# Hybrid attention block: earlier first products, head mix two tiles ahead, reordered GpSimd and load work around the switch of token halves

## The chip, the cores and the metric

The kernel runs on one core of a Trainium2 chip. The metric is device time in microseconds (us), the median of several executions. A core has a matrix engine (TensorE, PE in the rows; its weight loads are PEld), three engines for elementwise work (VectorE or DVE, ScalarE or ACT, GpSimd or POOL), and SyncE (SP, its queue is SPq), which here issues nearly all transfers between HBM and the on-chip memory. Each engine works through its own instructions in order. They meet only at semaphores: `wait_ge` holds an engine, and with it everything behind in its order, until a count is reached.

## The reference, cut to what matters

One layer on x, 2048 tokens of width 1024, all in float32:

- h = rmsnorm(x) times a gain; a projection with 2304 + 8 columns;
- eight heads of sliding window attention with sinks, and eight heads of causal attention with a cumulative forget gate, from these columns;
- x = x + mixed heads times w_out;
- h = rmsnorm(x) times a gain; u = relu(h w_up), 4096 wide; x = x + (u*u) w_down;
- a last rmsnorm.

Float32 accuracy is kept by splitting each operand of a product into a high part (rounded to the fast format) and the rest, and by three fast products: hi*hi, hi*lo, lo*hi. ScalarE makes each high part by a copy, VectorE makes the rest by a subtraction. The MLP uses a scheme of seven products of half blocks in place of eight, whose operands are sums and differences of blocks, made on GpSimd.

## The kernel before, in words

**Front (`project`, lines 182 to 653).** The 16 tiles of 128 tokens run through: load into a ring of four slots (line 318; slot reuse waits for the turn of the tile four before), square with sum on ScalarE (`square`, L399), two tiny operations on GpSimd for 1/rms (L384, L389), scaling on VectorE (`norm`, L477), eight transposes on TensorE (`turn`, L587), high copy on ScalarE in two halves (`split_ht_hi`, L405), rest on VectorE in two halves (`split_ht_lo`, L484). Four tiles make a token block b. The first two weight chunks of 128 columns give 8 products ("first products", `product_first`, L599), number n being chunk n % 2 on block n // 2, each 24 matmuls of 512 columns. They are put between the turns by `product_after_turn`: before the change numbers 0 to 5 stand after the turns of tiles 5, 7, 9, 11, 13, 15, and 6 and 7 at the end. Each result is read out by `split_first` on ScalarE (L425) and VectorE (L502), put one tile later. Product n waits for the rests of its four tiles; the turn of tile t waits for its scaling and for the rests of tile t-2. The gate weights (8 columns) are turned once (L615) at GATE_TILE. `square` runs one tile ahead, and its unused output goes to a scratch tile, `squares`.

**Head mix (`mix_out`, L1445 on).** Again 16 tiles: SyncE loads the two parts of the heads' output and the factors 1/sum (`load_mix`), GpSimd adds the parts (`join`, L1548), VectorE multiplies (`divide`, L1622), ScalarE and VectorE split (`split_mix`, L1585, L1627), TensorE does 48 matmuls (L1685), VectorE adds x (L1646), then square (L1608), 1/rms (L1570, L1573), scaling (L1653), turn (L1673), and ScalarE copies the turned tile out (`copy_ht`, L1596). From tile 8 on this copy goes to a staging tile that SyncE stores (`store_ht`, L1517), and GpSimd also forms token differences (L1560) in tiles 8 to 13. Two slots hold each of these tiles. SyncE's order in step t is: load_mix(t+2), wait for the add of t, store x_mid, load x(t+2), and from t = 9 store_ht(t-1).

**MLP (`feed`, L1725 on).** The up products go through 32 groups of 256 columns, 16 for each half of the tokens, with seven products (0 to 6) of 12 matmuls each (L2533). The operands of the seven products from the tokens are the "hops". Those of the first half are made at the start. Of the second half, numbers 4, 5 and 6 are made early, stored in HBM (`store_parts`) and loaded back in group 15 (`load_parts`, L1944), numbers 0 to 3 are split in group 15 (L2408). Weight operands are split three products ahead (LEAD = 3): ScalarE L2223, VectorE L2389. GpSimd makes four weight combinations per group (`mix_w` 1 to 4, L2085, L2090, L2092, L2096) and four result sums (`mix_u`, L2114 to L2124). VectorE's `add_up` (L2443) of product 5 stands behind the split of the next group's operand 0; product 6 waits for it: `pe.wait_ge(summed, 3 * g + 2)`. SyncE loads the weights of group g+2 (`load_w`, L1928) and stores seven results per group (L1948). LAST_TILE is the product ahead of which the turn of tile 15 stands.

Of the kernel before, what the change touches and what calls it, by code (L numbers as in the profile page):

```python
# [168 lines left out]
def project(nc, x, norm_mix, w_in, b_forget, sinks, ident_dram, causal_dram, alibi_dram, proj_hi, proj_lo, decay,  # L169
# [12 lines left out]
    with ExitStack() as ctx:  # L182
# [50 lines left out]

        squares = whole.raw["p_o_hi0"][:, S - D:S]
        gate_first = whole.raw["p_o_lo1"][0:G, S - D:S]
# [7 lines left out]
        assert NCH == 2 * PAIRS  # L243
        GATE_TILE = 7
        COPIED = 2 * ST + 1
# [3 lines left out]

        product_after_turn = {t: 2 * (t // TPB - 1) + t % TPB // 2 for t in range(TPB, ST) if t % 2}  # L250
        product_before_turn = {t + 1: n for t, n in product_after_turn.items() if t + 1 < ST}
# [142 lines left out]
        def _(act):  # L394
            def square(t):
                act.wait_ge(x_loaded[t % X_RING], 16 * (t // X_RING + 1))
                if t:
                    act.wait_ge(squared, t)
                nc.scalar.activation(squares, x_in[:, t % X_RING], ACT.Square,  # L399
                                     accum_out=ssum[:, t:t + 1]).then_inc(squared, 1)  # L400

            def split_ht_hi(t):
                for half in range(2):
                    act.wait_ge(turned, 2 * t + half + 1)
                    nc.scalar.activation(  # L405
                        ht_hi[half][:, :, t * P:(t + 1) * P],
                        ps_t[2 * (t % 2) + half].rearrange("p (k s) -> p k s", s=P),
                        ACT.Copy).then_inc(ht_hi_done, 1)
# [9 lines left out]
            def split_first(n):  # L418
                if n == 4:
                    act.wait_ge(squared, ST)  # L420
                split_o_hi(n % 2, n // 2, n % 4, n)
# [16 lines left out]

            square(0)
            for t in range(ST):  # L440
                if t + 1 < ST:
                    square(t + 1)
                if t in product_before_turn:
                    split_first(product_before_turn[t])
                split_ht_hi(t)
                if t == 2:
                    split_w_hi(0)
                    split_w_hi(1)
            for n in range(2 * SB - 3, 2 * SB - 1):
                split_first(n)  # L450
# [20 lines left out]
        def _(dve):  # L471
# [73 lines left out]
            for t in range(ST):  # L545
                if t + 1 < ST:
                    norm(t + 1)
                if t in product_before_turn:
                    split_first(product_before_turn[t])
                split_ht_lo(t)  # L550
                if t == GATE_TILE:
                    scale_gate_weights()
                if t == 2:
                    split_w_lo(0)
                    split_w_lo(1)
            for n in range(2 * SB - 3, 2 * SB - 1):
                split_first(n)
# [20 lines left out]
        def _(pe):  # L578
# [24 lines left out]
            def product_first(n):  # L603
                slot, b = n % 2, n // 2
                pe.wait_ge(ht_lo_done, 2 * TPB * (b + 1))
                pe.wait_ge(w_lo_done, 2)
                if n >= 4:
                    pe.wait_ge(o_lo_done, n - 3)
                product(slot, b, n % 4)
# [835 lines left out]
def mix_out(nc, o_main, o_rest, rsum_inv, x, norm_mlp, w_up, whole, joint, raw, w_raw, hop_hi, hop_lo, x_mid, h_rest,  # L1445
# [6 lines left out]
    with ExitStack() as ctx:  # L1452
# [91 lines left out]
        def _(pool):  # L1544
# [17 lines left out]
            pool.sem_inc(joined, 1)  # L1562
            pool.wait_ge(mhalf_set, 1)
            for t in range(ST):
                if t + 1 < ST:
                    join(t + 1)
                if t == ST - 1:
                    mlp.gpsimd_first(pool)
                pool.wait_ge(squared, t + 1)
                nc.gpsimd.tensor_scalar(rstd[:, t:t + 1], ssum[:, t:t + 1], 1.0 / D, EPS,  # L1570
                                        ALU.mult, ALU.add).then_inc(meaned, 1)
                pool.wait_ge(meaned, t + 1)
                nc.gpsimd.tensor_tensor(rstd[:, t:t + 1], rstd[:, t:t + 1], mhalf[:], ALU.pow).then_inc(rooted, 1)  # L1573
                if KEPT <= t < KEPT + 6:
                    mix_tokens(t - KEPT)
# [3 lines left out]
        def _(act):  # L1579
# [18 lines left out]

            act.sem_inc(mix_hi_done, 1)
            for t in range(ST):  # L1600
                if t + 1 < ST:
                    split_mix(t + 1)
                else:
                    mlp.scalar_first(act)
                act.wait_ge(added, HALVES * (t + 1))
                if t >= 2:
                    act.wait_ge(turned, 2 * (t - 1))
                nc.scalar.activation(xn[:, t % 2], xm[:, t % 2], ACT.Square,  # L1608
                                     accum_out=ssum[:, t:t + 1]).then_inc(squared, 1)
                if t:  # L1610
                    copy_ht(t - 1)
# [6 lines left out]
        def _(dve):  # L1618
# [12 lines left out]
            dve.sem_inc(divided, 1)  # L1631
            dve.sem_inc(mix_lo_done, 1)
            for t in range(ST):
                slot = t % 2
                if t + 1 < ST:
                    divide(t + 1)
                    split_mix(t + 1)
                else:
                    mlp.vector_first(dve)
# [8 lines left out]
                if t == 0:  # L1648
                    dve.wait_ge(gain_in, 16)
                if t == ST - 1:  # L1650
                    mlp.vector_second(dve)
                dve.wait_ge(rooted, t + 1)
                nc.vector.scalar_tensor_tensor(xn[:, slot], xm[:, slot], rstd[:, t:t + 1], gain[:],  # L1653
                                               ALU.mult, ALU.mult).then_inc(normed, 1)
                if t in SPLIT_AT:
                    n = SPLIT_AT.index(t)
# [68 lines left out]
def feed(nc, ctx, x_mid, h_rest, whole, joint, raw, raw_parts, w_raw, hop0_hi, hop0_lo, u_ops, b_kept, t_rest, t_parts,  # L1725
# [140 lines left out]
    hop_at = {0: (0, 4), 1: (0, 5), 3: (0, 6)}  # L1866
    LAST_TILE = 2
    hop_at |= {SWITCH + 1: (1, 0), SWITCH + 2: (1, 1), SWITCH + 5: (1, 2), SWITCH + 6: (1, 3),
# [51 lines left out]
    def sync(sp, store_last_tile):  # L1920
# [11 lines left out]
        def store_token_mix(n):  # L1932
            sp.wait_ge(t_mixed, 1 + 2 * (n + 1))
            sp.dma_start(t_rest[n], raw[:, 1]).then_inc(t_stored, 16)
# [72 lines left out]
        store_last_tile()  # L2007
        for g in range(GROUPS):
            if g:
                store_rest(g - 1)  # L2010
            if g + 2 < GROUPS:
                load_w(g + 2)
            if g == 1:
# [3 lines left out]
                sp.dma_start(raw[:], h_rest.rearrange("p j b k s -> p (j b) k s")).then_inc(raw_in, 16)  # L2017
            if g in rest_stored_at:
                store_token_mix(rest_stored_at[g])
            if g in pre_stored_at:  # L2020
                store_parts(pre_stored_at[g])
            if g == FG - 3:
                sp.wait_ge(t_stored, PRE_STORED)
                for slot, src in enumerate((h_rest[:, 0, 0], t_rest[T1_REST], t_rest[T2_REST], h_rest[:, 1, 0])):
                    sp.dma_start(raw[:, slot], src).then_inc(t_stored, 16)
            if g == FG - 1:
                for i in sorted(PRE_ORDER):
                    load_parts(i)
            if g == FG + 3:
# [76 lines left out]
    def gpsimd(pool):  # L2106
# [59 lines left out]
        for g in range(GROUPS):  # L2166
# [6 lines left out]
            if g == FG - 1:  # L2173
                pool.wait_ge(hop_lo_done, hop_count[1, 1])
            if g:
                mix_u(g - 1)
            if 2 <= g < 10:
                mix_rest(*divmod(g - 2, 2))
            if g + 1 < GROUPS:
                mix_w(g + 1, 3)  # L2180
        mix_u(GROUPS - 1)
# [498 lines left out]
```

## Time and profile before

| | us |
|---|---|
| median of 3 runs (2395.7 to 2396.91) | 2396.8 |
| profiled execution, its own time | 2394.05 |
| its span | 2392.4 |
| TensorE busy in the span | 2326.6 (97%) |
| VectorE busy | 1520.1 (64%) |
| ScalarE busy | 1154.1 (48%) |
| GpSimd busy | 706.9 (30%) |

The span runs from the first to the last instruction; the run's own time is 1.65 us more. TensorE leaves 65.8 us of the span idle, and the change works on places where it is idle.

### The profile page before, as it was taken

To read this page: it belongs to the slowest core of one execution; us is meant where nothing else is said; L and a number is where in the kernel's file an instruction comes from. 1 tells how busy PE (TensorE), PEld (TensorE's weight loads), DVE (VectorE), ACT (ScalarE), POOL (GpSimd) and SP (SyncE) were. 2 spreads that over 40 slices of the span, in tenths; PEclk is the share of its full clock that TensorE was granted. 3 is DMA by queue.
4 is the path that set the end of the run, shared out by engine and by line. 5 is a ranking of instruction groups with operands and counts; after the bars stand their busy time and mean duration, and the time that the engine had idled before them with its cause. 6 is when DMAs were issued, how large, how long until landed. Compare 5 with 4: busy or idle time off the path is not lost.

```text
span 2392.4 us, 34959 instructions
## 1 busy us (share of the span) xinstructions
PE 2326.6 (97%) x11346; PEld 1934.7 (81%) x11346; DVE 1520.1 (64%) x2623; ACT 1154.1 (48%) x2226; POOL 706.9 (30%) x593
## 2 busy tenths in 40 slices
PE   7999999999999998999899999999999999999998
PEld 5888888788888886887687877888888888888887
DVE  6588873688888886566745655444465555564454
ACT  5211112788888886223545555555553233333243
POOL 2000000111111114235568764666640032120132
PEclk9999999999999999999999999999999999999999
DMA  5567765666666565766455576654457486564464
GB/s 189 215 235 278 268 242 163 180 160 156 160 157 157 152 156 169 248 218 202 170 183 163 189 286 242 202 160 152 154 190 260 165 298 234 193 219 162 138 219 160
DMA packets 253970, 469.09 MB, mean 196 GB/s; under 512 B 59336, under 2 KB 119752, under 8 KB 246032
## 3 DMA queue, kind: packets, MB, share of 16 engines
q1 hardware_dynamic: 247808, 451.11, 58.6%
q0 software_dynamic: 6048, 16.52, 2.6%
q8 instruction: 64, 1.05, 0.2%
q14 instruction: 50, 0.41, 0.1%
HBM read 316.13 MB, written 151.42 MB: 195 GB/s over the span
## 4 chain that ended last, share of the span: by engine, by line
PE 51%; DVE 3%; POOL 2%; issue 2%; DMA 1%; ACT 1%; SPq 0%; POOLq 0%; ACTq 0%; DVEq 0%
PE m_ps L2533 24%; PE m_ps L2556 23%; PE m_ps L1685 4%; DMA b_kept<-f_kept 1%; POOL m_mix L1548 1%; DVE f_up_lo L2389 1%; PE m_ps L2574 0%; DVE m_xn L1653 0%; DVE m_xm L1646 0%; DVE m_mix L1622 0%; ACT m_mix_hi L1585 0%; DVE keep_lo L2408 0%; POOL h_raw L1560 0%; POOL f_kept L2157 0%; DVE hop_lo L1659 0%
## 5 line engine op out<-in xcount | busy, mean ns | idle before, releaser
L2556 PE MATMUL m_ps<-keep_hi,hop_hi 128*128 128x512 f32 x880 | 342.5, 389 | 0.4 <-DVE hop_lo L2392 0.4
L2556 PE MATMUL m_ps<-keep_hi,hop_lo 128*128 128x512 f32 x880 | 342.4, 389 | 0.0
L2556 PE MATMUL m_ps<-keep_lo,hop_hi 128*128 128x512 f32 x880 | 342.3, 389 | 0.0
L2392 DVE TENSOR_TENSOR hop_lo<-h_raw,hop_hi 128x512 fp32r<-128x512 f32 x224 | 176.6, 789 | 236.8 <-ACT hop_hi L2228 236.7
L2389 DVE TENSOR_TENSOR f_up_lo<-wide_raw,f_up_hi 128x512 fp32r<-128x512 f32 x160 | 182.5, 1142 | 223.0 <-ACT f_up_hi L2223 222.9
L2228 ACT ACTIVATE hop_hi<-h_raw 128x512 fp32r<-128x512 f32 x224 | 140.8, 630 | 334.4 <-PE m_ps L2556 330.5
L958 POOL DMA_DIRECT2D o_main<-a_o x63 | 36.5, 580 | 775.2 <-ACT a_o L1326 726.6
L599 PE MATMUL p_ps_o<-p_ht_lo,p_w_hi 128*128 128x512 f32 x576 | 224.5, 390 | 0.0
L2533 PE MATMUL m_ps<-keep_hi,f_up_hi 128*128 128x512 f32 x512 | 202.8, 396 | 6.1 <-DVE f_up_lo L2389 4.7
L2533 PE MATMUL m_ps<-keep_hi,f_up_lo 128*128 128x512 f32 x512 | 201.3, 393 | 0.0
L2533 PE MATMUL m_ps<-keep_lo,f_up_hi 128*128 128x512 f32 x512 | 199.4, 390 | 0.0
L2556 PEld LDWEIGHTS m_ps<-keep_hi,hop_hi 128*128 128x128 f32 x880 | 165.2, 188 | 34.8 <-DVE hop_lo L2392 0.8
L2556 PEld LDWEIGHTS m_ps<-keep_hi,hop_lo 128*128 128x128 f32 x880 | 165.2, 188 | 34.6
L2556 PEld LDWEIGHTS m_ps<-keep_lo,hop_hi 128*128 128x128 f32 x880 | 165.2, 188 | 34.3
L425 ACT ACTIVATE p_o_hi<-p_ps_o 128x512 fp32r<-128x512 f32 x70 | 41.8, 598 | 306.7 <-PE p_ps_o L599 299.4
L1199 DVE TENSOR_TENSOR a_pt_lo<-p_ps_o,a_pt_hi 128x512 fp32r<-128x512 f32 (+3 forms) x234 | 142.3, 614 | 15.3 <-ACT a_pt_hi L1313 14.6
L1313 ACT ACTIVATE a_pt_hi<-p_ps_o 128x512 fp32r<-128x512 f32 (+3 forms) x234 | 125.1, 544 | 41.1 <-PE p_ps_o L1085 36.0
L1022 PE MATMUL p_ps_x<-p_o_hi 128*128 128x512 f32 (+2 forms) x320 | 138.2, 432 | 4.4 <-DMA p_o_lo<-proj_lo 1.8
L1111 PE MATMUL p_ps_o<-a_pt_hi,a_v_fox 128*128 128x512 f32 (+1 forms) x320 | 128.9, 403 | 8.1 <-DVE a_pt_lo L1199 7.8
L599 PEld LDWEIGHTS p_ps_o<-p_ht_lo,p_w_hi 128*128 128x128 f32 x576 | 108.4, 188 | 22.4
L515 DVE CUSTOM_DVE_ANT_0 p_ps_x<-wide_raw,p_bias,p_rstd 128x1024 f32<-128x1024 f32 x86 | 116.1, 1350 | 14.8 <-DMA wide_raw<-gate_w 4.4
L2533 PEld LDWEIGHTS m_ps<-keep_hi,f_up_hi 128*128 128x128 f32 x512 | 96.6, 189 | 26.8 <-DVE f_up_lo L2389 7.3
(246 smaller groups left out, 5779.8 us busy)
## 6 DMA issues: line engine op xcount, KB each, us to landing
h_raw<-u_ops SPq DMA_DIRECT2D x224, 256.0 KB, 4.2
wide_raw<-in_w_up SPq DMA_DIRECT2D x32, 1024.0 KB, 7.2
u_ops<-f_u SPq DMA_DIRECT2D x128, 256.0 KB, 4.3
wide_raw<-in_x SPq DMA_DIRECT2D x59, 512.0 KB, 4.0
u_ops<-f_us SPq DMA_DIRECT2D x96, 256.0 KB, 2.3
proj_hi<-p_o_hi SPq DMA_DIRECT2D x17, 1024.0 KB, 6.2
proj_lo<-p_o_lo SPq DMA_DIRECT2D x17, 1024.0 KB, 8.3
h_raw<-in_w_down SPq DMA_DIRECT2D x58, 256.0 KB, 3.9
```

The source lines that it names most:

```text
L515: nc.vector.tensor_tensor_reduce(out=front.pair[:], in0=job_tile(m), in1=x_in[:, 2 + e], scale=rstd[:, t:t + 1], scalar=bias[:, g:g + 1], ...
L599: last = nc.tensor.matmul(ps_o[bank][:], w[:, slot, k, :], h, start=(k == 0 and n == 0), stop=(k == DK - 1 and n == 2))
L1022: last = nc.tensor.matmul(ps_s[ring][:, 0:w], tiles.q_fox[b // 2][:, q], kk[n // 2][:, k], start=(m == 0), stop=(m == 1 and n < b))
L1111: last = nc.tensor.matmul(bank[:, BANK - w:BANK], v_st[kind][:, step[2]], pt[:, 0:w], start=(first and pt is hi), stop=(last_one and pt is ...
L1199: nc.vector.tensor_tensor(pt_lo[i % PT_RING][:, 0:w], bank[:, 0:w], pt_hi[i % PT_RING][:, 0:w].bitcast(F32), ALU.subtract).then_inc(p_lo_d ...
L1313: nc.scalar.activation(pt_hi[i % PT_RING][:, 0:w], bank[:, 0:w], ACT.Copy).then_inc(p_hi_done, 1)
L1685: done = nc.tensor.matmul(joint.banks[2 * (t % 2) + half][:], m, w, start=(first and n == 0), stop=(last and n == 2))
L2228: nc.scalar.activation(op_tiles(m)[0], a_raw[:, q % A_RING], ACT.Copy).then_inc(op_hi_done, 1)
L2389: nc.vector.tensor_tensor(by_k(lo), w_part(m), by_k(hi).bitcast(F32), ALU.subtract).then_inc(op_lo_done, 1)
L2392: nc.vector.tensor_tensor(lo, a_raw[:, (m - UP) % A_RING], hi.bitcast(F32), ALU.subtract).then_inc(op_lo_done, 1)
L2533: last = nc.tensor.matmul(bank[:], w[:, k], h[i][:, k], start=(UP_OPENS[i] and k == 0 and m == 0), stop=(k == 3 and m == 2), skip_group_ch ...
L2556: last = nc.tensor.matmul(down_banks[b % 2][t][:], a[:, cols], w[j], start=(j == 0 and m == 0), stop=(j == FG - 1 and m == 2))
```

## The change

It has four parts. (1) Front: the first products 0 to 5 stand after the turns of tiles 3, 5, 8, 10, 12, 14; the squares of tiles 1 to 3 stand one place earlier in ScalarE's order; the split of the second weight chunk moves from tile 2 to tile 3; the scratch of the squares moves to another tile; the gate tile is 5. (2) Head mix: `join`, `divide` and `split_mix` work on tile t+2 in step t instead of t+1, and on VectorE and ScalarE they stand after the add and the square. (3) LAST_TILE is 3. (4) MLP: token mixes are stored ahead of the weight load; `load_parts(4)` stands at the head of group 15, parts 5 and 6 behind the result stores of group 14, and `load_w(17)` behind them; GpSimd's `mix_w` 3 stands ahead of the token differences, in group 15 also ahead of `mix_u`, which there waits for one hop more.

```diff
-        squares = whole.raw["p_o_hi0"][:, S - D:S]
+        squares = whole.raw["keep_hi"][:].rearrange("p (k b) s -> p k (b s)", k=DK // 2)[:, :, S - 2 * P:S]
-        GATE_TILE = 7
+        GATE_TILE = 5
-        product_after_turn = {t: 2 * (t // TPB - 1) + t % TPB // 2 for t in range(TPB, ST) if t % 2}
+        product_after_turn = {t: n for n, t in enumerate((3, 5, 8, 10, 12, 14))}
...
@@ scalar, front
+                if t == ST - 2:
+                    act.wait_ge(squared, ST)
...
             square(0)
+            square(1)
             for t in range(ST):
-                if t + 1 < ST:
-                    square(t + 1)
+                for ahead in range(t + 1, min(t + 3, ST)):
+                    if ahead == (t + 2 if ahead < X_RING else t + 1):
+                        square(ahead)
...
-                if t == 2:
-                    split_w_hi(0)
-                    split_w_hi(1)
-            for n in range(2 * SB - 3, 2 * SB - 1):
+                if t in (2, 3):
+                    split_w_hi(t - 2)
+            for n in range(2 * SB - 2, 2 * SB - 1):
@@ vector, front
-                if t + 1 < ST:
+                if t + 1 < ST and t != 3:
                     norm(t + 1)
...
+                if t in (2, 3):
+                    split_w_lo(t - 2)
+                if t == 3:
+                    norm(t + 1)
@@ tensor, front
-                pe.wait_ge(w_lo_done, 2)
+                pe.wait_ge(w_lo_done, min(n, 1) + 1)
@@ head mix, gpsimd
+            join(1)
             for t in range(ST):
-                if t + 1 < ST:
-                    join(t + 1)
+                if t + 2 < ST:
+                    join(t + 2)
@@ head mix, scalar
+            split_mix(1)
             for t in range(ST):
-                if t + 1 < ST:
-                    split_mix(t + 1)
-                else:
+                if t == ST - 1:
                     mlp.scalar_first(act)
...
+                if t + 2 < ST:
+                    split_mix(t + 2)
                 if t:
                     copy_ht(t - 1)
@@ head mix, vector
+            divide(1)
+            split_mix(1)
             for t in range(ST):
-                if t + 1 < ST:
-                    divide(t + 1)
-                    split_mix(t + 1)
...
+                if t + 2 < ST:
+                    divide(t + 2)
...
+                if t + 2 < ST:
+                    split_mix(t + 2)
@@ MLP
-    LAST_TILE = 2
+    LAST_TILE = 3
@@ MLP, sync
         for g in range(GROUPS):
+            if g == FG - 1:
+                load_parts(4)
             if g:
                 store_rest(g - 1)
+            if g in rest_stored_at:
+                store_token_mix(rest_stored_at[g])
+            if g == FG - 1:
+                load_parts(5)
+                load_parts(6)
             if g + 2 < GROUPS:
                 load_w(g + 2)
...
-            if g in rest_stored_at:
-                store_token_mix(rest_stored_at[g])
...
-            if g == FG - 1:
-                for i in sorted(PRE_ORDER):
-                    load_parts(i)
@@ MLP, gpsimd
             if g == FG - 1:
-                pool.wait_ge(hop_lo_done, hop_count[1, 1])
+                mix_w(g + 1, 3)
+                pool.wait_ge(hop_lo_done, hop_count[1, 2])
             if g:
                 mix_u(g - 1)
+            if g + 1 < GROUPS and g != FG - 1:
+                mix_w(g + 1, 3)
             if 2 <= g < 10:
                 mix_rest(*divmod(g - 2, 2))
-            if g + 1 < GROUPS:
-                mix_w(g + 1, 3)
```

## Rows read from the trace of the kernel before

**Rows 1.** TensorE's waits: who was waited for, us in total, times, longest
```profile
PE p_ps_x L587 <- DVE wide_raw L477: 16.7, 6, 8.3
PE m_ps L1685 <- DVE m_mix_lo L1627: 5.6, 6, 1.4
```

**Rows 2.** Timeline of TensorE, front: start, length, instruction, [idle before, releaser]
```profile
26.97 0.78 PE L599 MATMUL p_ps_o<-keep_hi,p_w_hi 128*128 128x512 f32 x1
...
33.51 1.91 PE L587 MATMUL p_ps_x<-ident,wide_raw 128*128 128x128 f32 x16
36.37 1.03 PE L615 MATMUL p_ps_x<-ident,a_causal 128*8 128x128 f32 x8 [0.95 <-DVE p_ht_lo L484]
...
42.70 1.91 PE L587 MATMUL p_ps_x<-ident,wide_raw 128*128 128x128 f32 x16
```

**Rows 3.** Timeline of ScalarE, front
```profile
16.39 1.99 ACT L416 ACTIVATE p_w_hi<-p_w_raw 128x1024 fp32r<-128x1024 f32 x2
18.29 1.05 ACT L399 ACTIVATE p_o_hi_raw<-wide_raw 128x1024 f32<-128x1024 f32 x1
...
77.21 0.60 ACT L425 ACTIVATE p_o_hi<-p_ps_o 128x512 fp32r<-128x512 f32 x1 [4.84 <-PE p_ps_o L599]
...
82.65 0.60 ACT L425 ACTIVATE p_o_hi<-p_ps_o 128x512 fp32r<-128x512 f32 x1 [3.89 <-PE p_ps_o L599]
```

**Rows 4.** Timeline of VectorE, front
```profile
16.43 1.29 DVE L477 SCALAR_TENSOR_TENSOR wide_raw<-wide_raw,p_rstd,p_gain 128x1024 f32<-128x1024 f32 x1 [1.05 <-POOL p_rstd L389]
...
46.45 1.29 DVE L477 SCALAR_TENSOR_TENSOR wide_raw<-wide_raw,p_rstd,p_gain 128x1024 f32<-128x1024 f32 x1 [1.03 <-POOL p_rstd L389]
```

**Rows 5.** Two windows: busy us (instructions) by engine, granted clock, transfer share, GB/s
```profile
19.00:28.00 9.00, 4.61 (x19) 4.02 (x20) 7.51 (x9) 5.81 (x13) 4.57 (x6) 0.50 0.37 130
1467.00:1484.00 17.00, 12.48 (x46) 9.19 (x44) 5.18 (x8) 5.66 (x11) 11.87 (x8) 0.90 1.02 417
```

**Rows 6.** Timeline of VectorE, head mix
```profile
1037.21 0.69 DVE L1646 TENSOR_TENSOR m_xm<-m_ps,m_x_in 128x512 f32<-128x512 f32 x1 [1.55 <-PE m_ps L1685]
...
1049.09 0.69 DVE L1646 TENSOR_TENSOR m_xm<-m_ps,m_x_in 128x512 f32<-128x512 f32 x1 [1.56 <-PE m_ps L1685]
...
1064.75 3.43 DVE L1653 SCALAR_TENSOR_TENSOR m_xn<-m_xm,m_rstd,m_gain 128x1024 f32<-128x1024 f32 x1 [2.13 <-POOL m_rstd L1573]
...
1126.42 1.28 DVE L1646 TENSOR_TENSOR m_xm<-m_ps,m_x_in 128x512 f32<-128x512 f32 x2
```

**Rows 7.** Timeline of SyncE's issues, head mix, step 9
```profile
1064.81 0.65 SPq L1517 DMA_DIRECT2D h_rest<-m_stage  x1
...
1067.51 1.38 SPq L1506 DMA_DIRECT2D m_inv<-rsum_inv  x2
```

**Rows 8.** Landing of the transfers of L1506 issued from 1064 to 1070
```profile
DMA to landing us min/median/max: 6.3/6.5/6.7
```

**Rows 9.** Timeline of GpSimd, MLP, groups 4 and 15
```profile
1251.95 2.40 POOL L2143 TENSOR_TENSOR h_raw<-h_raw 128x1024 f32<-128x1024 f32 x1 [12.08 <-DMA t_rest<-h_raw]
...
1453.67 1.68 POOL L2114 TENSOR_TENSOR f_us<-f_u 128x512 f32<-128x512 f32 x1 [5.17 <-DVE keep_lo L2408]
...
1469.40 1.66 POOL L2085 TENSOR_TENSOR f_s<-wide_raw 128x512 f32<-128x512 f32 x1 [0.96 <-DMA wide_raw<-in_w_up]
```

**Rows 10.** Timeline of TensorE, MLP: groups 4 and 16
```profile
1258.49 0.47 PE L2533 MATMUL m_ps<-keep_hi,f_up_hi 128*128 128x512 f32 x1 [1.37 <-ACT f_u L2282]
...
1479.23 0.47 PE L2533 MATMUL m_ps<-f_hop_hi,f_up_hi 128*128 128x512 f32 x1 [1.98 <-DVE f_up_lo L2389]
...
1484.18 0.47 PE L2533 MATMUL m_ps<-f_hop_hi,f_up_hi 128*128 128x512 f32 x1 [0.38 <-issue]
```

**Rows 11.** Timeline of VectorE, group 15: hop 2
```profile
1457.54 4.56 DVE L2408 TENSOR_TENSOR keep_lo<-h_raw,keep_hi 128x1024 fp32r<-128x1024 f32 x2
```

**Rows 12.** Timeline of SyncE's issues, group 15
```profile
1461.88 0.45 SPq L1928 DMA_DIRECT2D wide_raw<-in_w_up  x1
...
1463.66 0.81 SPq L1944 DMA_DIRECT2D f_hop_hi<-t_parts  x1
```

More of the change, by code:

```diff
@@ L398, in square @@
                     act.wait_ge(squared, t)
-                nc.scalar.activation(squares, x_in[:, t % X_RING], ACT.Square,
+                nc.scalar.activation(squares, x_in[:, t % X_RING].rearrange("p (k c) -> p k c", k=DK // 2), ACT.Square,
                                      accum_out=ssum[:, t:t + 1]).then_inc(squared, 1)
             def split_ht_hi(t):
+                if t == ST - 2:
+                    act.wait_ge(squared, ST)
                 for half in range(2):
@@ L418, in split_first @@
             def split_first(n):
-                if n == 4:
-                    act.wait_ge(squared, ST)
                 split_o_hi(n % 2, n // 2, n % 4, n)
@@ L552, in _ @@
                     scale_gate_weights()
[L553 to L556, printed above, removed]
+                if t in (2, 3):
+                    split_w_lo(t - 2)
+                if t == 3:
+                    norm(t + 1)
+            for n in range(2 * SB - 2, 2 * SB - 1):
                 split_first(n)
@@ L1632, in _ @@
             dve.sem_inc(mix_lo_done, 1)
+            divide(1)
+            split_mix(1)
             for t in range(ST):
                 slot = t % 2
-                if t + 1 < ST:
-                    divide(t + 1)
-                    split_mix(t + 1)
-                else:
+                if t == ST - 1:
                     mlp.vector_first(dve)
```

## The prediction

> **What bounds the kernel now.** I read the busy shares first: TensorE is busy for 2326.6 of 2392.4 us, so what an edit is worth is what it does to 65.8 us of idle TensorE, and to the clock. Then the waits of TensorE by stage [rows 1]: 16.7 us in six waits of the front for scaled tiles, 5.6 us in six waits of the head mix for split mixes. The timelines of the MLP add two places: 1.37 us in group 4, and the waits of group 16 for products 5 and 6 [rows 10]. Last I followed each engine's order around these places, since every part of the change moves waits that stand behind one another.
>
> **Front, the start.** Today the first product starts at 26.97 [rows 2], behind six turns. It now needs four tiles. The scaling of tile 3 began at 16.43 after 1.05 us of waiting for its square [rows 4]; with squares further ahead that goes, and turn 3 comes at about 16.7 instead of 17.7 (16.43 + 1.29). ScalarE then has weight chunk 0 (half of 1.99, from 16.39), the square of tile 4 (1.2 with its read) and two half copies of about 0.5: 19.6 [rows 3]. VectorE's second rest follows, 0.6, plus about 0.1 of hand-over: product 0 starts at 20.4, 6.6 us earlier. But turns 4 and 5 now come after it. 16 transposes last 1.91 [rows 2], about 0.2 of it under the matmul behind them, so 1.7 us come back: gain 4.9.
>
> **Front, what opens later.** Call P1 the end of product 1 (42.70 today). ScalarE's read-out of product 1 stands ahead of the copies of the next tile and the square of the one after, and the scaling that needs this square ends at 46.45 + 1.29 = 47.74, P1 + 5.0 [rows 4]. Today TensorE covers this with two turns and a product (7.2 us). After the change product 2 stands behind three turns: turns 6 and 7 take 1.7, and turn 8 needs the scaling, so it starts at P1 + 5.1: 3.4 us idle. Product 2 needs the rests of tile 7, 1.2 us behind that scaling on VectorE: 0.4 more beyond turn 8. Product 4 (tiles 8 to 11) now stands behind turns 11 and 12, product 6 behind turn 15 alone. From the end of a product to the rests of the next tile it is 36.37 - 33.51 = 2.86 us [rows 2], less 0.1; behind two turns that leaves 1.1 idle, behind one 1.9. Sum of new idle 6.8. So 6.8 - 4.9 = 1.9 us of loss.
>
> **Front, the clock.** Today's clock is 0.50 from 19 to 28, the 1.2 GHz level, although 16 transposes ran in it, and the first product paid 33.51 - 26.97 = 6.54 against 82.65 - 77.21 = 5.44 [rows 2, 3, 5]: 1.1 us. In the new order TensorE stands from 17.7 to 20.4, so I let product 0 run mostly at the low level, 2.4 us dearer than at the high one (at most 5.4, were it low throughout; it cost 1.1 today behind two turns, and here none precede it). Idle of 3.4 us ahead of turn 8 may drop it again; other drops here follow idle of 2 to 4 us, each costs 1.5 to 1.8; I take 0.8 as an expected share. Net clock: 2.4 - 1.1 + 0.8 = 2.1. The front loses 4.0; with no drop at all 1.9 - 1.1 = 0.8, at worst 5.2. By the Trainium skill (TensorE: Matmul & The Clock Gate, Part 4: PE-mode transpose) transposes don't count as activity of the clock gate like matmuls; the trace agrees at 19 to 28. By that rule a product ahead of the turns is no worse off for clock than one behind them, and the front would lose nearer 3.
>
> The rest of the front costs nothing: the gate turn keeps its 0.95 idle one tile earlier, and the strided scratch is on ScalarE, which idled 4.84 and 3.89 us ahead of the last read-outs [rows 3].
>
> **Head mix.** The 8th step's add ends at 1049.09 + 0.69 = 1049.78, the 14th's at 1126.42 + 1.28 = 1127.70 [rows 6]: 77.9 us for six tiles. A tile without waits is 1049.09 - 1037.21 = 11.88 [rows 6], six are 71.3. So 6.6 to 6.7 us are there, from the chain add, square, root, scaling (with GpSimd's operations alongside it takes 3.43 where it takes 1.29 alone, rows 4, 6), divide, split. With mixes two ahead this chain no longer gates TensorE.
>
> What takes its place: from step 9 on a ring through all engines. load_mix(t+3) stands behind store_ht(t-1) in SyncE's order; that waits for copy_ht(t-1), now behind split_mix(t+2), behind divide(t+2), behind join(t+2), behind load_mix(t+2). Today from the issue of the store to the landing of the last load it is 1067.51 + 0.7 + 6.7 - 1064.81 = 10.1 us [rows 7, 8], with the store of x_mid and a load of x still in the queues; behind an idle queue I estimate 8.2 (2.1 MB at the rate of about 310 GB/s of these loads, and the latency). Then join 2.4 (same shape as the first row of [rows 9]), divide 1.3, high part 1.1, copy 1.0: a lap of 14.1 against a tile of 11.87. The loads of mix 11, with no store ahead of them yet, land 10.1 us behind add 8, so join ends 0.6 behind add 9, and divide, high part and copy put store_ht(8) 4.2 behind it. Each lap adds 2.3: 6.5, 8.7, 10.9. In step 12 the rests of mix 14 are ready 11.2 to 13.6 us behind the add, where 12.0 is needed, and the add itself stands behind them. Steps 13 and 14 then give back 2.9 to 5.3. Net gain 1.4 to 3.8; I take 2.2. With a lap of 16 (the 10.1 of today) the ring costs more than it gives, a loss of 4; with no ring the gain is 6.7. In tiles 0 to 7 nothing stores, and the 11.87 is kept.
>
> **LAST_TILE**: TensorE's order changes, but VectorE's chain of hop splits sets this stretch: 0, between -0.5 and +0.5.
>
> **Group 4.** The difference waits 12.08 us for the store of a token mix behind a 1 MB load; weight combination 3 stands behind it, and TensorE waits 1.37 [rows 9, 10]. Both edits lift that: gain 1.4.
>
> **Group 15 and 16.** Today product 5 of group 16 starts when part 5 has landed (1479.23), product 6 with part 6 (1484.18), and the next group 2.85 later, 1487.03 [rows 10]. Without waits that would be 1480.0, so 7.0 us are there. Part 4 is now issued when product 4 of group 15 ends, 1455.3, and is out of the way. Parts 5 and 6 stand behind the result stores of group 14, so behind `mix_u(14)`. That starts today at 1453.67 [rows 9]; it now waits for hop 2. This one took 4.56 against GpSimd and ended at 1462.1 [rows 11]; undisturbed it takes 2.35 but starts about 1.3 later, since combination 3 falls into hops 0 and 1: 1461.2. Four sums of 1.3 to 1.8, against hop 3: done near 1468 (earliest 1466.5). So part 5 is issued at about 1468.8, against 1463.66 [rows 12]. Then 0.5 MB of stores and 4.2 MB of parts at 417 GB/s [rows 5] end near 1481.
>
> And group 17's weights, issued at 1461.88 and landed at 1469.40 today [rows 9, 12], now come behind the parts: 1 MB more, 3 us: 1484. ScalarE reads them in the step of product 4 of group 16; VectorE's split waits for that, its add for product 5 stands behind the split, and product 6 waits for this add. 1484 + 0.6 + 0.7 + 0.7 + 0.1 = 1486.1 against 1484.18: loss 1.9. TensorE has then stood some 7 us, and its 12 matmuls begin at the low level, 1.5 more (a wait of 1.98 was enough today, 1479.23 to 1483.8 for a product of 2.75). Loss 3.4; I take 3.2. Earliest: combinations at 1466.5, weights at 1481, loss 0.5. Worst 6. Were the weights not to gate, product 6 would start with part 6 near 1479.5: gain 4.7. By the Trainium skill (SBUF — State Buffer, SBUF: two separate sides) GpSimd and a VectorE operation with two SBUF inputs exclude one another for the whole instruction; the 3.43 against 1.29 agrees. By it the four sums would end nearer 1469, and the loss be about 1 us more.
>
> **Sum**: front +4.0, head mix -2.2, group 4 -1.4, group 16 +3.2: 3.6 us slower. The profiled run's 2394.05 would become 2397.7; it lies 2.75 under the median, and on the median I forecast 2396.8 + 3.6 = **2400.4**. 0.2%, which is about what a measurement tells from no change, is 4.8 us, so this is most likely within it.
>
> **Rivals.**
> 1. *The late weights don't gate product 6* (2392.5). If the queues serve the weights beside the parts, they land before 1478 and group 16 gains 4.7: 4.0 - 2.2 - 1.4 - 4.7 = -4.3, faster. It decides from a landing earlier than 1479.5 - 2.1 = 1477.4. For it: DMA shares rows by 16 engines. Against: today parts 5 and 6, issued back to back, landed 5 us apart, one behind the other [rows 10]. Chance 0.12.
> 2. *The ring of the head mix doesn't close* (2395.9): landing in under 6 us; the full 6.7: -0.9. Against: the issues alone take 3.7. Chance 0.13.
> 3. *The ring turns in 16* (2406.6): head mix loses 4.0 instead of gaining 2.2: +9.8. For it: 10.1 measured. Against: the two transfers ahead of it will be gone. Chance 0.14.
> 4. *The front breaks even and group 16 loses little* (2395.0): no low clock, 0.8, and 0.5: -2.3 with the other parts. Chance 0.08.
> 5. 1 and 2 together, about 2388: 0.05.
> The forecast has 0.48, between 2397.5 and 2403.5 by its own bounds.
>
> Range: 2390 to 2406.5, leaving out rival 5, half of 3 and the ends of the rest. Faster (below 2392.0): rival 5, 0.07 of rival 1 and 0.04 of rivals 2 and 4, 0.16. Slower (above 2401.6): rival 3 and 0.20 of the forecast, 0.34. Within: 0.50.
>
> **What would show it.** Front: first product near 20.4, a wait of some 3.4 us ahead of turn 8, the last first product read near 86.6 (82.65 today). Head mix: steps 9 to 11 at 11.87, then waits for L1627 in steps 12 to 14, SyncE's h_rest issues later behind their add by 2 us each. Group 4 without wait. Group 16: L1928 landing behind L1944, L2443 of product 5 behind the split, product 6 after 1484. Wrong it is if turn 8 follows turn 7 without wait, or if the weights land ahead of part 6.

## The result, and the profile after

The changed kernel takes 2411.63 us (median of 4 runs, 2411.1 to 2412.94) against 2396.86 for the kernel before: ratio 1.0063, 95% interval [1.0048, 1.0078]. It is 14.8 us slower, where 3.6 were forecast with a range up to 2406.5. The direction was right; the size was wrong by a factor of four. The two profiled executions are 2392.4 and 2409.6 us long, 17.2 apart; the one of before lies 2.8 under its median, so the traces show some 2.4 us more than the medians. One execution of a kernel below took 8259.9 us instead of some 2420, and it is left out of that kernel's median.

The clearest way to find where such a difference arises is to take one instruction at the end of each stage in both traces and to watch how far apart the two are:

| | before | after | apart | in this stage | forecast |
|---|---|---|---|---|---|
| last first product read out (L425, L426) | 82.65 | 88.73 | +6.08 | +6.1 | +4.0 |
| first matmul of the head mix | 940.77 | 946.91 | +6.14 | 0 | 0 |
| product 6 of group 0 | 1166.15 | 1178.73 | +12.58 | +6.4 | -2.2 |
| next idle place, group 9 | 1380.94 | 1391.74 | +10.80 | -1.8 | -1.4 |
| matmul behind product 6 of group 16 | 1487.03 | 1504.10 | +17.07 | +6.3 | +3.2 |

From there on nothing changes (17.2 apart at the last matmul). So one stage has the wrong sign, the head mix, and two cost more than forecast.

**The front after.** TensorE's timeline, to be held against [rows 2]: the columns are start, length, instruction and, in brackets, idle before it and who ended it.

```profile
20.73 0.50 PE L602 MATMUL p_ps_o<-keep_hi,p_w_hi 128*128 128x512 f32 x1 [2.09 <-DVE p_ht_lo L486]
...
42.23 1.71 PE L590 MATMUL p_ps_x<-ident,wide_raw 128*128 128x128 f32 x8 [3.18 <-DVE wide_raw L479]
...
60.26 0.50 PE L602 MATMUL p_ps_o<-keep_hi,p_w_hi 128*128 128x512 f32 x1 [0.86 <-DVE p_ht_lo L486]
...
75.91 0.50 PE L602 MATMUL p_ps_o<-keep_hi,p_w_hi 128*128 128x512 f32 x1 [1.80 <-DVE p_ht_lo L486]
```

Four stretches of the same trace. Behind the length stand the busy us of PE, PEld, DVE, ACT and POOL, then the granted clock (1.00 is 2.4 GHz, 0.50 is 1.2 GHz), the share of transfers and GB/s:

```profile
20.70:22.00 1.30, 1.27 (x6) 1.05 (x7) 1.18 (x2) 1.13 (x3) 0.09 (x1) 1.00 0.56 227
22.00:25.40 3.40, 3.40 (x10) 2.63 (x9) 2.53 (x3) 0.00 (x0) 1.56 (x2) 0.51 0.04 16
42.20:46.00 3.80, 3.77 (x14) 3.29 (x15) 3.56 (x5) 2.23 (x4) 0.81 (x4) 0.55 0.34 102
75.90:80.00 4.10, 4.09 (x11) 3.27 (x12) 0.00 (x0) 0.00 (x0) 0.00 (x0) 0.60 0.92 339
```

The first product starts at 20.73, and the idle times of 3.18, 0.86 and 1.80 us stand where the working put them. But three products run partly at the low level: product 0, product 2 behind the wait of 3.18, and product 6 behind that of 1.80.

**The head mix after.** TensorE's waits from 946 to 1156 us (us in total, times, longest), against [rows 1]:

```profile
PE m_ps L1681 <- DVE m_xn L1659: 7.7, 3, 4.2
PE m_ps L1693 <- DVEq L1637: 2.4, 1, 2.4
PE m_ps L1693 <- DVE m_mix_lo L1632: 1.5, 1, 1.5
```

One lap of the ring, step 10 to 11, engine by engine: SyncE's stores with the last loads behind one of them, GpSimd's join and root, VectorE's divide and scaling, ScalarE's high copy and turned copies.

```profile
1072.62 0.66 SPq L1520 DMA_DIRECT2D h_rest<-m_stage  x1
...
1088.08 0.64 SPq L1520 DMA_DIRECT2D h_rest<-m_stage  x1
...
1090.59 1.13 SPq L1509 DMA_DIRECT2D m_inv<-rsum_inv  x2
...
1103.44 0.64 SPq L1520 DMA_DIRECT2D h_rest<-m_stage  x1
...
1120.05 0.64 SPq L1520 DMA_DIRECT2D h_rest<-m_stage  x1
```

```profile
1097.69 2.40 POOL L1551 TENSOR_TENSOR m_mix<-m_mix,m_rest 128x1024 f32<-128x1024 f32 x1 [8.64 <-DMA m_inv<-rsum_inv]
1100.17 1.23 POOL L1574 TENSOR_SCALAR m_rstd<-m_ssum 128x1 f32<-128x1 f32 x1
```

```profile
1100.12 1.23 DVE L1627 TENSOR_TENSOR m_mix<-m_mix,m_inv 128x1024 f32<-128x1024 f32 x1 [6.52 <-POOL m_mix L1551]
1102.07 3.39 DVE L1659 SCALAR_TENSOR_TENSOR m_xn<-m_xm,m_rstd,m_gain 128x1024 f32<-128x1024 f32 x1 [0.72 <-POOL m_rstd L1577]
```

```profile
1101.38 1.06 ACT L1589 ACTIVATE m_mix_hi<-m_mix 128x1024 fp32r<-128x1024 f32 x1 [6.59 <-DVE m_mix L1627]
1102.35 1.07 ACT L1600 ACTIVATE m_stage<-m_ps 128x512 f32<-128x512 f32 x2
```

The lap is 1103.44 - 1088.08 = 15.4 us; the one before it took 15.5, the next ones 16.6 and 15.8. Of this lap 9.6 us go from the store's issue to the join, and 5.8 us through the engines, as worked out. The tiles of these steps take about what a lap takes: the turns of tiles 10 to 13 start at 1091.05, 1105.51, 1122.09 and 1138.00, which is 14.5, 16.6 and 15.9 us apart.

**Group 16 after**, against [rows 10, 12]: the weights of group 17 and part 5 on SyncE, the first readers of these weights, and TensorE.

```profile
1480.19 0.46 SPq L1952 DMA_DIRECT2D f_hop_hi<-t_parts  x1
...
1482.45 0.43 SPq L1936 DMA_DIRECT2D wide_raw<-in_w_up  x1
```

```profile
1496.79 0.63 ACT L2234 ACTIVATE f_up_hi<-wide_raw 128x512 fp32r<-128x512 f32 x1 [13.43 <-DMA wide_raw<-in_w_up]
```

```profile
1497.45 1.17 DVE L2400 TENSOR_TENSOR f_up_lo<-wide_raw,f_up_hi 128x512 fp32r<-128x512 f32 x1 [12.77 <-ACT f_up_hi L2234]
1498.55 0.68 DVE L2454 TENSOR_TENSOR f_u<-m_ps,f_u 128x512 f32<-128x512 f32 x1
```

```profile
1488.44 0.47 PE L2544 MATMUL m_ps<-f_hop_hi,f_up_hi 128*128 128x512 f32 x1 [1.86 <-issue]
...
1499.37 0.77 PE L2544 MATMUL m_ps<-f_hop_hi,f_up_hi 128*128 128x512 f32 x1 [6.67 <-DVE f_u L2454]
```

The chain is the forecast one: weights, ScalarE, VectorE's split, its add, product 6. The first matmul of the product takes 0.77 instead of 0.47, and the granted clock from 1499.3 to 1502 is 0.50: the low level again.

### The profile page after: what moved, and what is told of

It is laid out like the page before. It is cut to its first block, busy times and chain, and to the rows that moved or that the text cites. A ratio compares the mean times of both kernels' runs of the same rounds, so it can differ in the third digit from the quotient of the medians.

```text
span 2409.6 us, 34959 instructions
## 1 busy us (share of the span) xinstructions
PE 2333.6 (97%) x11346; PEld 1939.0 (80%) x11346; DVE 1485.6 (62%) x2623; ACT 1155.2 (48%) x2226; POOL 715.9 (30%) x593
## 4 chain that ended last, share of the span: by engine, by line
PE 51%; DMA 3%; DVE 3%; POOL 1%; issue 1%; SPq 1%; ACT 0%; POOLq 0%; ACTq 0%; DVEq 0%
PE m_ps L2544 23%; PE m_ps L2567 23%; PE m_ps L1693 4%; DMA m_inv<-rsum_inv 2%; DMA b_kept<-f_kept 1%; DVE f_up_lo L2400 1%; POOL m_mix L1551 1%; DMA wide_raw<-in_w_up 1%; DVE keep_lo L2419 0%; PE m_ps L2585 0%; SPq L1506 0%; DVE m_mix L1627 0%; PE m_ps L1681 0%; POOL f_kept L2167 0%; DVE hop_lo L2419 0%
## 5 line engine op out<-in xcount | busy, mean ns | idle before, releaser
L2400 DVE TENSOR_TENSOR f_up_lo<-wide_raw,f_up_hi 128x512 fp32r<-128x512 f32 x160 | 165.3, 1035 | 230.5 <-ACT f_up_hi L2234 230.3
L426 ACT ACTIVATE p_o_hi<-p_ps_o 128x512 fp32r<-128x512 f32 x70 | 41.9, 598 | 314.1 <-PE p_ps_o L602 306.8
L602 PE MATMUL p_ps_o<-keep_hi,p_w_hi 128*128 128x512 f32 x288 | 114.9, 399 | 4.7 <-DVE p_ht_lo L486 4.7
```

The source lines that it names most:

```text
L602: last = nc.tensor.matmul(ps_o[bank][:], w[:, slot, k, :], h, start=(k == 0 and n == 0), stop=(k == DK - 1 and n == 2))
L2400: nc.vector.tensor_tensor(by_k(lo), w_part(m), by_k(hi).bitcast(F32), ALU.subtract).then_inc(op_lo_done, 1)
```

## The experiments

Times are medians; the ratios are to runs of the kernel before on the same chip, and the differences to the changed kernel are to the 2411.63 above. The stretch from the last read-out of the front to the first matmul of the head mix, in which no run changes anything, lasted between 857.5 and 862.0 us over the traces, whatever the kernel; so stages are read from the traces by their own length, and medians only for the whole.

**Each part alone on the kernel before.** The edits are the front of the diff, its head mix with LAST_TILE, and its MLP part.

> The kernel before with the front part of the change alone. Theory A (the losses lie where the two traces differ and don't depend on one another): the last first product is read out near 88.7 instead of 82.65, the rest of the kernel is the one before, so +6.1 us, about 2403. Of it 3.2, 0.9 and 1.8 us are idle ahead of turn 8, product 4 and product 6, against 5.5 us gained by the earlier start, and the rest is matmuls at the low clock behind these idle times. Rival B: part of the 6.1 us comes back later (the weight chunks or their stores are what the projection waits for), so less than +3.

Measured: 2402.34 against 2397.18 us, ratio 1.0021 [1.0011, 1.0031]. From the first turn to the last read-out the front takes 78.4 us against 74.4 before. The idle times are 3.19, 0.86 and 1.80 as with the whole change, yet here product 6 ran at the high level and 1.6 us less are lost. Over seven traces of the changed front this length is 78.4 to 81.9 us, over five of the old one 73.5 to 74.4; the means are 6.4 apart, so the 4.0 of this pair is the smallest cost of the front that was seen.

> The kernel before with the head mix two tiles ahead and LAST_TILE 3 alone. Theory A: the ring through load, join, divide, high copy, turned copy and store closes from tile 9 on and turns once in about 16 us: +6.4 us, about 2403; TensorE waits for the scaling in steps 11 to 13. Rival B: the ring closes only because the rest of the kernel was shifted against the transfers: less than +3.

Measured: 2402.86, ratio 1.0024 [1.0015, 1.0034]. The turns of steps 10 to 13 stand 14.97, 16.49 and 16.13 us apart. Theory A holds: the ring closes without the rest of the change, and TensorE waits 2.93, 2.78 and 2.30 us for the scaling.

> The kernel before with the MLP part alone (both edits). Theory A: -1.8 us in group 4 and +6.4 us in group 16, where the weights of group 17 land behind the parts and gate product 6: +4.6 us, about 2401.5. Rival B: group 16 costs less where the token mixes come by the old schedule: between -2 and +2.

Measured: 2400.18, ratio 1.0018 [1.0006, 1.0031]. In its trace group 4 gains 1.8 us, as with the whole change (from the matmul behind product 6 of group 0 to the idle place in group 9 it is 211.95 us before, 210.2 in both), and product 6 of group 16 waits longer than with the whole change, 7.07 us:

```profile
1487.91 0.76 PE L2536 MATMUL m_ps<-f_hop_hi,f_up_hi 128*128 128x512 f32 x1 [7.07 <-DVE f_u L2446]
```

The three medians are 5.2, 5.7 and 3.0 us above before, together 13.8 of the 14.8 us. Within what such medians can tell, the parts add up.

**The ring cut at ScalarE.**

```diff
-                if t + 2 < ST:
-                    split_mix(t + 2)
                 if t:
                     copy_ht(t - 1)
+                if t + 2 < ST:
+                    split_mix(t + 2)
```

> The changed kernel with one swap on ScalarE in the head mix: the turned copy of tile t-1 stands ahead of the high copy of tile t+2, so the store no longer waits for the divided mix and the ring is cut there. Theory A (the ring): all tiles at 11.87 us, the 11.8 us of excess of steps 9 to 14 go: about 2400 (11 to 12 us under the changed kernel). Theory B (the transfers themselves can't keep up, about 10 us from the store to the last landing and then GpSimd, VectorE behind): the lap stays above 12 and less than half of it comes back, above 2405. Theory C (the scaling standing behind the divide is the loss by itself, ring or none): the excess stays in part, about 2404.

Measured: 2401.58, ratio to before 1.0024 [1.0014, 1.0034], 10.0 us under the changed kernel; it still has its front and its group 16. Fourteen tiles in a row stand 11.87 us apart, and TensorE's waits from 949 to 1150 us are

```profile
PE m_ps L1693 <- DVEq L1637: 2.4, 1, 2.4
PE m_ps L2544 <- ACT f_u L2293: 1.9, 1, 1.9
PE m_ps L1693 <- DVE m_mix_lo L1632: 0.3, 1, 0.3
```

The wait of 7.7 us for the scaling is gone, and from the first matmul of the head mix to group 9 it is 431.9 us instead of 444.8. Transfers, joins and divides are the same as in the changed kernel, and from the store's issue to the join it still takes 9.6 to 10.3 us; only what the store waits for has changed. So theory B falls: the transfers can keep up.

**The ring cut at SyncE**, with ScalarE's order as changed.

```diff
                 if 3 <= t + 2 < ST:
                     load_mix(t + 2)
+                if t - 1 > KEPT:
+                    store_ht(t - 2)
...
-                if t > KEPT:
-                    store_ht(t - 1)
+            store_ht(ST - 2)
```

> The changed kernel with a second cut of the ring, on SyncE instead of ScalarE: in each step the store of a turned tile stands behind the loads of the next mix, one step later than now. ScalarE's order is as changed. Theory A (the ring store, load, join, divide, high copy, turned copy): tiles at 11.87 us throughout, 11 to 12 us faster, about 2400, as with the other cut. Theory D (what helped before was that ScalarE's turned copy came earlier, whatever the loads do): less than 4 us faster, above 2407.

Measured: 2401.37, ratio 1.0026 [1.0016, 1.0036]. Tiles at 11.87 us throughout. Two cuts at different places give the same time, and here ScalarE's turned copy comes no earlier in its order: theory D falls. Both cuts also make the joins early, so theory C (the scaling held behind the divide) needs a run of its own.

**Is it the ring, or the scaling held behind a late join?** TensorE's wait names the scaling. Here GpSimd's root of tile t stands ahead of `join(t + 2)`, and VectorE's `divide(t + 2)` behind the scaling of t.

```diff
@@ gpsimd
-                if t + 2 < ST:
-                    join(t + 2)
...
                 nc.gpsimd.tensor_tensor(rstd[:, t:t + 1], ..., ALU.pow).then_inc(rooted, 1)
+                if t + 2 < ST:
+                    join(t + 2)
@@ vector
-                if t + 2 < ST:
-                    divide(t + 2)
...
                 if t + 2 < ST:
+                    divide(t + 2)
                     split_mix(t + 2)
```

> The changed kernel with, in the head mix, GpSimd's root of tile t ahead of the join of tile t+2 and VectorE's divide of tile t+2 behind the scaling of tile t, so that a late mix no longer holds the scaling. Theory A (the ring sets the pace by itself): laps stay near 15.5 us from tile 9 on, TensorE now waits for the mix rests instead of the scaling, 1 to 4 us faster, about 2409. Theory C (the scaling held behind join and divide is the larger part of the loss): 6 us or more, about 2405.

Measured: 2425.95, ratio 1.0118 [1.0102, 1.0133], 14 us slower than the changed kernel; both theories expected a gain. The stores, the divide and TensorE's wait in its trace:

```profile
1076.40 0.66 SPq L1520 DMA_DIRECT2D h_rest<-m_stage  x1
...
1094.62 0.64 SPq L1520 DMA_DIRECT2D h_rest<-m_stage  x1
...
1113.07 0.64 SPq L1520 DMA_DIRECT2D h_rest<-m_stage  x1
```

```profile
1107.63 3.35 DVE L1627 TENSOR_TENSOR m_mix<-m_mix,m_inv 128x1024 f32<-128x1024 f32 x1 [6.23 <-POOL m_mix L1551]
```

```profile
PE m_ps L1692 <- DVE m_mix_lo L1632: 19.3, 5, 5.6
```

The scaling is early now, and TensorE waits for the mix rests instead. The divide meets GpSimd's token difference, which used to lie beside the scaling, and takes 3.35 instead of 1.23 us; that and 10.1 to 10.6 us from store to join make the four laps 18.0 to 18.5 us, and the four slow tiles take 17.0 to 19.4. So with the scaling out of the way the tile still follows the lap, and the loss does not need a held scaling: the ring suffices as the cause. What the held scaling would cost at an unchanged lap this run does not show, since the edit made the lap longer too. My figure for this run was wrong because I moved the divide onto the difference.

**The front: pairs of turns ahead of each product.**

```diff
-        product_after_turn = {t: n for n, t in enumerate((3, 5, 8, 10, 12, 14))}
+        product_after_turn = {t: n for n, t in enumerate((3, 5, 7, 9, 11, 13))}
```

> The changed kernel with the first products 0 to 5 behind the turns of tiles 3, 5, 7, 9, 11, 13 instead of 3, 5, 8, 10, 12, 14. Theory A (idle time is what the turns between two products don't cover): two turns ahead of each of products 2, 4 and 6, so about 0.9 us idle ahead of each instead of 3.2, 0.9 and 1.8, and no product behind the first at the low clock: the front ends 6 us earlier than in the changed kernel, about 2405.5. Rival B: product 2 now waits for the rests of tile 7, which are as late as the scaling of tile 8 was: less than 2 us earlier.

Measured: 2420.36 (three executions), ratio 1.010 [1.008, 1.012], 8.7 us slower than the changed kernel. In the traces the front is 5.7 us longer (85.9 against 80.2); the other 3.8 lie in the unchanged stretch behind it, 862.0 against 858.2, and are within its spread. TensorE now waits 4.38 us ahead of products 2 and 4 each and 2.13 ahead of product 6 (four waits in all):

```profile
PE p_ps_o L602 <- DVE p_ht_lo L486: 13.0, 4, 4.4
```

Rival B was right, more than it said. By the kernels' orders, the read-out of a product stands ahead of the copies of the next tile on ScalarE, so after each odd product the next two tiles' copies, squares, scalings and rests run one behind the other, and a product that needs the second of them waits for the whole chain however the turns are dealt out. In the kernel before, product 2 needs nothing that is made behind product 1.

> The changed kernel with the squares of all tiles two places ahead in the front, not of the first four alone. Theory A (the square behind the read-out of a product is part of the chain that turn 8 and products 4 and 6 wait for): about 1 us less idle ahead of each, 3 us, and perhaps no product at the low clock: 3 to 6 us faster, about 2407. Rival B (VectorE's order, the scaling behind the rests of the tile before, sets the same times): within 1 us.

Measured: 2414.1, ratio 1.0059 [1.004, 1.0077]. The idle time ahead of turn 8 falls from 3.18 to 2.05, those of 0.86 and 1.80 stay, and 1.9 us are lost ahead of product 0, which now waits 3.96. Nothing is gained: rival B in sum, A in one place of three.

**Group 15: the weights ahead, or the sums early.** In the first, `load_w(g + 2)` stands ahead of `load_parts(5)`; in the second GpSimd waits for `hop_count[1, 1]` again.

> The changed kernel with the weights of group 17 loaded ahead of parts 5 and 6 in group 15. Theory A (the weights behind the parts gate product 6): they land some 8 us earlier, product 5 waits some 3 us longer for part 5, product 6 then waits for part 6 only: 2 to 3 us faster, about 2409. Theory B (the late result sums are the cause, and the order behind them matters little): within 1 us of the changed kernel.

> The changed kernel with GpSimd's result sums of group 14 waiting for hop 1 as before, not for hop 2; all else as changed. Theory B (the late sums hold the stores, and the stores the loads): sums, stores and loads come 5 to 6 us earlier, product 6 with them: 5 to 6 us faster, about 2406. Theory A (the place of the weights behind the parts): the weights still land last and gate product 6, less than 3 us faster.

Measured: 2410.59, ratio 1.0064 [1.0048, 1.0081], and 2409.44, ratio 1.0052 [1.0035, 1.0068]. Whole medians hardly tell these apart from the changed kernel; the traces do. From the idle place in group 9 to the last matmul it is 1004.5 us before, 1010.9 changed, 1006.7 with the weights first, 1006.7 with the early sums. Each cure gives 4.2 back. With the weights first the one long wait is that of product 5, 5.80 instead of 1.86 us, because part 5 now lands behind the weights; product 6 follows it without a wait:

```profile
1495.46 0.76 PE L2544 MATMUL m_ps<-f_hop_hi,f_up_hi 128*128 128x512 f32 x1 [5.80 <-issue]
```

With the early sums it is still product 6 that waits:

```profile
1498.50 0.76 PE L2544 MATMUL m_ps<-f_hop_hi,f_up_hi 128*128 128x512 f32 x1 [6.21 <-DVE f_u L2454]
```

With the weights first the add no longer gates product 6, with the early sums it still does, only earlier. Up to the end of group 16 the first gives 3.8 back and the second 5.4; of the latter some 1.2 are lost again to an idle time at 2065 us that lies outside the edit. Neither theory is alone: late sums delay the whole queue, and the weights at its end decide.

**What gains, together.** First with the front of the pairs, then with the front of the kernel before; both have the ring cut at ScalarE, LAST_TILE 3, the edits of group 4, and group 15 as before.

> A kernel of the parts that should gain: front with products behind turns 3, 5, 7, 9, 11, 13; head mix two ahead with the turned copy ahead of the high copy; both edits of group 4; group 15 as in the kernel before. If the parts add up: front -1 to -3, head mix -6 to -7, group 4 -1 against the kernel before: 8 to 11 us under it, about 2387.5. If they don't: above 2392.

Measured: 2401.72, ratio 1.0024 [1.0014, 1.0034]. Its front alone takes 12 us more than before; without that it would be 2390.

> Only what gained in the runs so far, on the kernel before: head mix two ahead with the turned copy ahead of the high copy, LAST_TILE 3, both edits of group 4; front and group 15 as before. By the stages of the traces so far: 7.2 us from the stretch between the first matmul of the head mix and group 9 (432.1 against 439.25 with the edits of group 4) and 1 us from group 4: 8 us under the kernel before, about 2389. Rival: the gain is eaten in group 16, whose waits shift with the arrival of the transfers: 2393 or more.

Measured: **2387.84 us** (2385.88 to 2388.44), ratio 0.9955 [0.9942, 0.9969], 8.9 us under the kernel before and 23.8 under the changed one. From the first matmul of the head mix to group 9 it takes 432.1 us against 440.2, and from there to the last matmul 1005.5 against 1004.5.

> e9 with group 15 as in the changed kernel, but the weights of group 17 ahead of parts 5 and 6 and the result sums waiting for hop 1. Theory A (the two cures of group 15 add up, since one brings all loads forward and the other takes the weights out from behind the parts): 2 us or more under e9. Rival B (each cure alone already reached the limit set by 4 MB of parts and weights): within 1 us of e9, or behind it.

Measured: 2389.9, ratio 0.9966 [0.9952, 0.9979]. From group 9 to the end 1003.5 us against 1005.5 in e9, but the median isn't lower: no difference that these runs can show. Rival B.

## Why the prediction was wrong

- **Front, start and idle times: right.** First product at 20.4 forecast, 20.73 measured; 3.4, 1.1 and 1.9 us against 3.18, 0.86 and 1.80; the wait of 0.4 ahead of product 2 didn't show.
- **Front, the clock: mis-sized.** I had a net of 2.1 us. Product 0 took 7.19 us, 0.65 over the 6.54 of [rows 2] and not 1.3; but turn 8 with product 2 lost 1.6 and product 6 another 1.7 (7.2 instead of 5.44). I gave "0.8 as an expected share" to drops behind idle times; in this trace two happened. The sum is 4.0 instead of 2.1, and the front +6.1 instead of +4.0. The front-only trace, without the drop at product 6, has +4.0; over all traces the front costs 6.4. The rule on transposes that the prediction cites would, as worked out there, have made product 0 no dearer than before; it was 0.65 dearer. These traces don't decide on the rule: before the change the clock is 1.00 from 8 to 17 us and 0.50 from 22 to 27, with only turns in both stretches, so "the trace agrees" was said of one of the two.
- **Head mix: the step that failed.** The ring was named with every link, and its first store is where it was forecast (4.4 us behind the add of step 9, forecast 4.2). What failed is "behind an idle queue I estimate 8.2", against 9.7, 9.6, 10.9 and 10.1 measured in the four laps from the store's issue to the join. A transfer cost of 2.1 MB and a latency was put in the place of a measured 10.1 [rows 7, 8], on the ground that two transfers ahead of it would go. They no longer stand ahead, but that gave back at most half a us: SyncE alone takes 3.0 us from the store's issue to that of the last load, and this one lands 6.0 to 7.8 us later. Nor does the queue stay idle, since the next store of x_mid and load of x now follow the last load by 4.3, 2.5, 1.3 and 1.3 us; the two laps in which they follow closest have the 10.9 and the 10.1. So the lap was 15.4 to 16.6, not 14.1, and over four laps the 2.2 us of gain became 6.4 of loss. It was rival 3, whose 4 us were too few as well: in it I let the first late mix cost nothing, while step 10's store was already 8.0 behind its add instead of 6.5. In the trace this step is 8.6 of the 13.6 us by which the forecast was short. What the prediction said of the stage without a ring was right: with the ring cut and the old front, the stretch from the first matmul of the head mix to the one behind product 6 of group 0 is 6.3 us shorter than before (221.9 against 228.2), where 6.7 were forecast.
- **A gate that the working left out.** With GpSimd's join of t+2 ahead of its root of t, a late mix holds the scaling. It is what TensorE's wait shows, but the run with the root first shows the loss without it.
- **LAST_TILE: right.** From the turn of tile 14 to product 6 of group 0 it is 28.48 us in both kernels (1137.67 to 1166.15, 1150.25 to 1178.73).
- **Group 4: right**, -1.8 for -1.4, in the trace of the whole change and in that of its MLP part alone.
- **Group 16: right in mechanism, mis-sized.** Counted with the 10.8 us that the trace then lags, the sums start at 1461.0 (forecast 1461.2), part 5 is issued at 1469.4 (1468.8), and the weights are read at 1486.0 (1484). They landed 14.3 us after their issue. Product 6 started 2.5 later than worked out, and its low clock cost 1.9 instead of 1.5: +6.3, beyond my worst of 6. Over all traces, from group 9 to the last matmul it is 1004.0 to 1006.4 us with the old group 15 and 1010.5 to 1012.3 with the changed one, so a difference of 5.5 between the middle ones is the fairer figure.
- **Chances.** The three errors have one sign. Their terms were not independent, since in these traces late transfers brought idle time and idle time brought the low clock; so a range made of one term's bounds at a time (up to 2406.5) was too narrow above. Rival 4's own parts add up to 2394.5, not 2395.0.

## What to carry to other kernels

When work is formed further ahead, follow the buffer's ring once round through every queue, and price each link with a measured duration, however disturbed; an estimate of what it would be undisturbed is worth its difference only if a trace shows the undisturbed case. Where the lap exceeds the tile by little, one swap that takes an unrelated store or copy out of the ring can be worth more than the whole advance: here 10 us for two lines. A product that starts early can start a wait elsewhere, if its successors are made in an order that the product's own read-out heads.

## What the runs showed of the hardware

- After four turns and 2.09 us idle the first product began at a granted clock of 1.00 and fell to 0.51 only 1.3 us into it. I had it low from its start. With the same 1.80 us idle ahead of product 6 the clock fell in one execution (0.89 as the mean of 75 to 90 us) and not in another (1.00, the front-only run):

```profile
75.00:90.00 15.00, 13.69 (x60) 11.37 (x61) 3.87 (x6) 2.39 (x4) 0.00 (x0) 1.00 0.53 185
```

- VectorE's operations grow when GpSimd's two-input ones run beside them: the divide 1.23 to 3.35, the scaling 1.29 to 3.43 [rows 4, 6]. That agrees with the Trainium skill (SBUF — State Buffer, SBUF: two separate sides), by which the two exclude one another. Moving a VectorE operation within a step moves who pays this, as the run with the root first showed.
- A 0.5 MB store and the four loads behind it took about the same whether a store of x_mid and a load of x stood some 2 us ahead of them (10.1 us from the store's issue to the last landing, before) or followed them (9.6 to 10.9 us to the join, after).
